# Heads of the blocks in a two-layer f32 kernel: weights split across block ends, the second unit's low part by GpSimd, and the norm's root later

## The reference, cut to what matters

```python
def rms_norm_2(x, g):
    xf = x.astype(jnp.float32)
    y = xf * lax.rsqrt(jnp.mean(xf * xf, axis=-1, keepdims=True) + EPS)
    return (y * g.astype(jnp.float32)).astype(x.dtype)

def swiglu(h, w_gate, w_up, w_down):
    return (jax.nn.silu(h @ w_gate) * (h @ w_up)) @ w_down
```

## Time and profile before

| | us |
|---|---|
| median of three runs | 1918.85 |
| the profiled execution | 1918.93 |
| its span, first to last instruction | 1917.1 |
| PE busy in the span | 1732.8 (90%) |
| DVE busy | 1429.0 (75%) |
| ACT busy | 612.9 (32%) |
| POOL busy | 371.2 (19%) |

### The profile page before, as it was taken

How to read it: one execution, slowest core, us unless ns; L and a number is a source line. 1 busy time by engine, 2 the same in 40 slices (tenths; PEclk the granted TensorE clock), 3 DMA queues, 4 the chain that set the end, 5 groups by cost and what they waited for, 6 DMA issues and landing times.

```text
span 1917.1 us, 25162 instructions
## 1 busy us (share of the span) xinstructions
PE 1732.8 (90%) x9676; PEld 1319.2 (69%) x9676; DVE 1429.0 (75%) x2702; ACT 612.9 (32%) x798; POOL 371.2 (19%) x324
## 2 busy tenths in 40 slices
PE   6999988777787877878999998999999999989999
PEld 4788853333333323336999898899989997779998
DVE  7887789888888888877888778655565656866554
ACT  2135331010100011002643413554454444455452
POOL 0002145444445444451000054000000000000000
PEclk9999999998989898899999999999999999999999
DMA  9856599999999999996545453554545454444543
GB/s 394 317 204 234 196 393 409 422 422 421 422 421 421 422 422 416 421 398 259 190 170 201 162 198 111 186 188 177 194 165 192 176 190 155 153 155 153 186 178 118
DMA packets 68600, 508.57 MB, mean 265 GB/s; under 512 B 7777, under 2 KB 12129, under 8 KB 15969
## 3 DMA queue, kind: packets, MB, share of 16 engines
q0 software_dynamic: 37008, 268.98, 34.0%
q1 hardware_dynamic: 25920, 230.45, 32.6%
q10 hardware_dynamic: 5584, 7.98, 1.3%
HBM read 505.28 MB, written 6.29 MB: 267 GB/s over the span
## 4 chain that ended last, share of the span: by engine, by line
PE 62%; DMA 15%; DVE 15%; ACT 2%; issue 2%; POOL 2%; ACTq 1%; SPq 0%; DVEq 0%; POOLq 0%
PE PB L943 24%; PE PB L954 11%; PE PB L925 11%; DMA arena<-in_uv,eidx 9%; DMA ring<-in_uv,eidx 6%; PE PB L1129 2%; PE PB L666 2%; PE PB L737 2%; DVE arena L1758 1%; PE PB L618 1%; PE PB L723 1%; PE PB L834 1%; DVE gu_lo L1312 1%; PE PB L970 1%; PE PB L856 1%
## 5 line engine op out<-in xcount | busy, mean ns | idle before, releaser
L925 PE MATMUL PB<-arena 128*128 128x512 f32 x604 | 304.9, 663 | 96.5 <-DVE arena L1780 96.5
L943 PE MATMUL PB<-h_hi,gu_hi 128*128 128x256 f32 x1344 | 377.6, 281 | 3.5 <-DVE gu_lo L1846 3.4
L943 PE MATMUL PB<-h_hi,gu_lo 128*128 128x256 f32 x1344 | 376.9, 280 | 0.0
L943 PE MATMUL PB<-h_lo,gu_hi 128*128 128x256 f32 x1344 | 375.8, 280 | 0.0
L925 PEld LDWEIGHTS PB<-arena 128*128 128x128 f32 x604 | 125.2, 212 | 275.0 <-issue 149.6
L2775 POOL DMA_INDIRECT arena<-in_uv,eidx x193 | 225.7, 1170 | 319.5 <-PE PB L925 218.5
L1758 DVE CUSTOM_DVE_ANT_0 arena<-arena,XN 128x1024 f32<-128x1024 f32 x187 | 222.9, 1222 | 60.8 <-DMA arena<-in_uv,eidx 60.7
L943 PEld LDWEIGHTS PB<-h_hi,gu_hi 128*128 128x128 f32 x1344 | 254.1, 189 | 8.0 <-DVE gu_lo L1846 5.1
L943 PEld LDWEIGHTS PB<-h_lo,gu_hi 128*128 128x128 f32 x1344 | 252.0, 188 | 2.8
L943 PEld LDWEIGHTS PB<-h_hi,gu_lo 128*128 128x128 f32 x1344 | 252.7, 188 | 0.0
L1846 DVE TENSOR_TENSOR gu_lo<-ring,gu_hi 128x2048 fp32r<-128x2048 f32 x84 | 192.5, 2292 | 16.4 <-ACT gu_hi L2514 14.4
(11 more groups left out here) (460 smaller groups left out, 2974.1 us busy)
## 6 DMA issues: line engine op xcount, KB each, us to landing
ring<-in_ffn SPq DMA_DIRECT2D x88, 1536.0 KB, 6.7
arena<-in_ada SPq DMA_DIRECT2D x24, 768.0 KB, 8.1
ring<-in_qkv SPq DMA_DIRECT2D x12, 1024.0 KB, 4.7
ring<-in_zg SPq DMA_DIRECT2D x8, 1024.0 KB, 4.9
ring<-in_ada SPq DMA_DIRECT2D x4, 1536.0 KB, 13.8
ring<-in_up SPq DMA_DIRECT2D x4, 1024.0 KB, 4.8
ring<-in_wo SPq DMA_DIRECT2D x4, 1024.0 KB, 6.6
ring<-in_pq SPq DMA_DIRECT2D x4, 1024.0 KB, 4.8
```

Of the source, the lines that this page charges most:

```text
L925: mm = pe.matmul(PB[2 + 2 * t + h][:, :], lhsT=diag(n), rhs=uv[n % UVB][:, 1, h * 512:(h + 1) * 512], start=False, stop=False, skip_group_ ...
L943: mm = pe.matmul(PB[j % 2][:, b * T:(b + 1) * T], lhsT=w[:, j % 2, o:o + P], rhs=h[:, k, :], start=(k == 0 and m == 0), stop=(k == DC - 1 ...
```

## The change

1. **Weights split on across block ends.** ACT casts the next block's units 0 and 1 behind the silus of the last two units (`next_block`, `lead_next_block(f, j)`); behind a mixer it casts unit 1 when the mixer's last output unit is done. DVE makes unit 0's low part ahead of the last unit's `scale_gate`, no longer behind the last `activation`.
2. **The second unit's low part by POOL** (`split_second`, `trail` in the POOL program) in ffn1, ffn2, ffn3, S5 and the attention mixer. In ffn0 DVE still makes it, now ahead of the sum of squares.
3. **Activations first.** ACT writes all of `h_hi`, then squares, then takes the root (ffn0: casts unit 1 between). DVE makes all of `h_lo`, then `norm_sums`, the inverse root and the diagonals.
4. **The root's row inside the second unit.** PE makes it between the gate's half and the up half of gate_up(1) (not for S5, where its place is kept). DVE makes the down weights' low part of unit 0 ahead of keeping the row.
5. The first two and last four units of ffn1 to ffn3 are written out, so the loop holds 16.

```diff
-                root_row(n, 6)
-                rolled = LOOPS if f else 0
+                gate_up(1, between=lambda: root_row(n, 6))
+                down(0)
+                gate_up(2)
+                down(1)
...
             def head(n):
 
+                split_pairs(n, 0, 1, 2, 3)
                 norm_sums(n)
-                split_pairs(n, 0, 1)
                 norm_root(n)
-                split_pairs(n, 2)
-                if n in DG:
-                    diagonals()
-                split_pairs(n, 3)
+                diagonals()
...
                 else:
-                    split_pairs(n, 0, 1)
+                    split_pairs(n, 0, 1, 2, 3)
+                    split_gate_up(1)
                     norm_sums(n)
-                    split_pairs(n, 2, 3)
                     norm_root(n)
                     diagonals()
-                split_gate_up(1)
                 link(v.tensor_scalar(stat[:, 12:14], stat[:, 6:8], 0.5, None, ALU.mult))
+                split_down(0)
                 keep_root_row(n, 6)
...
+                    if j == FU - 2:
+                        if f == 0:
+                            trail("s5in", 0)
+                        elif f == 1:
+                            split_next_block(2)
+                        elif f == 2:
+                            trail("qkv", 0)
                 dve.wait_ge(a_done, a0 + FU + 2)
...
+            def head(n):
+
+                tell(s.activation(stat[:, 14:15], ones[:, 0:1], ACT.Sqrt), act_link)
+                split_h(n)
+                square(n)
+                norm_root(n)
...
                 if f == 0:
                     tell(s.activation(stat[:, 14:15], ones[:, 0:1], ACT.Sqrt), act_link)
-                    split_h(n, 3)
+                    split_h(n)
                     act.wait_ge(uv_used, TT * NSLOT)
+                    lead_gate_up(1)
+                    norm_root(n)
...
                     if j + 2 < FU:
                         lead_gate_up(j + 2)
+                    else:
+                        next_block(j + 2 - FU)
...
-            act.wait_ge(unit_done, UNIT[("s5out", 2)] + 1)
-            lead_next_block(1)
+            for j in range(2):
+                act.wait_ge(unit_done, UNIT[("s5out", 2 + j)] + 1)
+                lead_next_block(1, j)
...
+            def split_second(f):
+
+                pool.wait_ge(gu_hi_done, FU * f + 2)
+                pool.wait_ge(gu_lo_done, FU * f + 1)
+                g.tensor_tensor(gu_lo[:, 1, :], ring[:, (ffn_base[f] + 1) % NS, 0:2 * D], gu_hi[:, 1, :].bitcast(F32),
+                                ALU.subtract).then_inc(gu_lo_done, 1)
+                pool.wait_ge(gu_lo_done, FU * f + 2)
```

More of the change, by code:

```diff
@@ L939, in gate_up @@
                     for b in range(2):
+                        if b:
+                            between()
                         for k in range(DC):
@@ L983, in ffn @@
                 clear(3)
-                root_row(n, 6)
-                rolled = LOOPS if f else 0
-                if rolled:
-                    with pe.Fori(0, rolled) as i:
-                        for j in range(NS):
+                gate_up(1, between=lambda: root_row(n, 6))
+                down(0)
+                gate_up(2)
+                down(1)
+                if f:
+                    with pe.Fori(0, ROUNDS) as i:
+                        for j in range(2, 2 + NS):
                             gate_up(j + 1, i)
                             down(j, i)
-                for j in range(rolled * NS, FU):
+                for j in range(2 + ROUNDS * NS if f else 2, FU):
                     if j + 1 < FU:
@@ L1873, in ffn @@
                 else:
-                    split_pairs(n, 0, 1)
+                    split_pairs(n, 0, 1, 2, 3)
+                    split_gate_up(1)
                     norm_sums(n)
-                    split_pairs(n, 2, 3)
                     norm_root(n)
                     diagonals()
-                split_gate_up(1)
                 link(v.tensor_scalar(stat[:, 12:14], stat[:, 6:8], 0.5, None, ALU.mult))
+                split_down(0)
                 keep_root_row(n, 6)
[L1882 to L1885, removed]
+                scale_gate(0)
+                activation(0)
+                dve.wait_ge(gu_lo_done, a0 + 2)
+                split_gate_up(2)
+                scale_gate(1)
+                split_down(1)
+                activation(1)
+                if f == 0:
+                    s5_tables(1)
+                split_gate_up(3)
+                if f:
+                    with dve.Fori(0, ROUNDS) as i:
+                        for j in range(2, 2 + NS):
                             scale_gate(j, i)
@@ L2522, in silu, with next_block @@
                     s.activation(act_gs[:, j % 2, :], act_gs[:, j % 2, :], ACT.Silu).then_inc(silu_done, 1)
+                def next_block(j):
+                    if f == 1:
+                        lead_next_block(2, j)
+                    elif f < 3:
+                        lead(("s5in", None, "qkv")[f], j, a_done, FU * (f + 1) + 1 + j)
                 if f == 0:
                     tell(s.activation(stat[:, 14:15], ones[:, 0:1], ACT.Sqrt), act_link)
[L2527 removed]
+                    split_h(n)
                     act.wait_ge(uv_used, TT * NSLOT)
[L2529 to L2536 removed]
+                    lead_gate_up(1)
+                    norm_root(n)
+                else:
+                    head(n)
+                if f:
+                    for j in range(2):
+                        lead_down(j)
+                        silu(j)
+                        lead_gate_up(j + 2)
+                    with act.Fori(0, ROUNDS) as i:
+                        for j in range(2, 2 + NS):
                             lead_down(j, i)
@@ L2539, in ffn @@
                             lead_gate_up(j + 2, i)
-                for j in range(rolled * NS, FU):
+                for j in range(2 + ROUNDS * NS if f else 0, FU):
                     lead_down(j)
@@ L2718, in _ @@
             lead("mo", 3, unit_done, UNIT[("mo", 1)] + 1)
-            act.wait_ge(unit_done, UNIT[("mo", 2)] + 1)
-            lead_next_block(3)
+            for j in range(2):
+                act.wait_ge(unit_done, UNIT[("mo", 2 + j)] + 1)
+                lead_next_block(3, j)
             ffn(3)
```

89 lines of the change are left out of this document (32 added, 57 removed).

## The result

The changed kernel takes 1925.8 us (median of 6 executions) against 1918.9 for the kernel before; the ratio is 1.0042, with an interval of 1.0031 to 1.0054. It is slower, as forecast (1924.8, range 1920.0 to 1928.3). The profiled execution took 1925.62 us with a span of 1923.8; before it was 1918.93 and 1917.1.

What follows compares the result with a forecast made beforehand. PE carries 62% of the chain; only its waits in the heads were taken to matter. Terms 4.36 + 1.75 + 1.75 - 0.7 - 0.7 - 0.6 = +5.86 on 1918.93 give 1924.8 us, range 1920.0 to 1928.3.

Steps and rivals of the forecast that it cites:

- ffn0's scaled gate: ffn0's head: DVE's new order moves the scaled gate from 898.10 to 902.46, +4.36 us, and gate_up(3) with it.
- Either way this costs nothing more: ffn0: whether or not POOL's zeroing holds the a_hi cast, PE's chain ends inside gate_up(3)'s start at 922.2; 0 extra.
- The rival on the clock: PE idling ahead of ffn0's down(0) and ffn1's and ffn3's first matmuls lowers its clock: +3.3 us, 1928.1; chance 0.10.
- PE's row is ready by then: ffn0: PE's root row inside gate_up(1) is ready when DVE's down weights' subtraction ends at 902.00, adding no delay.
- ffn1 and ffn3, +1.75 each: Heads of ffn1 and ffn3: ACT's unit 1 cast, table load and small root go ahead of h_hi; +1.75 us each.
- S5, ffn2, attention: -0.7, -0.7, -0.6: Heads of S5, ffn2 and attention: PE's next work starts earlier by 0.7, 0.7 and 0.6 us.
- POOL's low part: 0: Second unit's low part on POOL, taken as 5.1 us, ends before gate_up(1) needs it in ffn1; worth 0.
- the shared-port rival: POOL's new subtraction meeting DVE's sum of squares would cost up to 1.2 us a head; within the range, no chance given.
- The thin covers: Around the row in gate_up(1) and unit 2's low part, work stays hidden by 0.2 and 0.15 us; otherwise some tenths per head.

Runs made afterwards that it cites:

- ffn0_row_ahead: Changed kernel with ffn0's new order kept on DVE and ACT, but PE's root row ahead of gate_up(1): 1923.2 us, ratio 1.0029.
- ffn0_row_inside: Changed kernel with ffn0's old order on DVE and ACT only, PE's root row staying inside gate_up(1): 1924.7 us, ratio 1.0028.
- memset_later: Changed kernel with POOL's zeroing in ffn0 waiting for a_done 1, a count already met, so the zeroing did not move: 1925.1 us, ratio 1.0035.
- zeroing_behind_a: Changed kernel with POOL's zeroing in ffn0 behind a_lo of unit 0, by the right count (a_done 3): 1927.4 us, ratio 1.0033.
- gains_alone: Changed kernel with the heads of ffn0, ffn1 and ffn3 put back to the old order; S5, ffn2 and attention heads stay changed: 1916.4 us, ratio 0.9982.
- gains_split: gains_alone with only ACT's 16 transfers in ffn0 parted in eight and eight: 1914.8 us, ratio 0.9981.
- gains_zero_split: gains_alone with two edits in ffn0, the zeroing behind a_lo of unit 0 and ACT's 16 transfers parted in eight and eight: 1912.7 us, ratio 0.9963.

## Why the prediction was right, step by step

- **ffn0's scaled gate**, +4.36: measured +4.26. The subtraction began at 893.70 + 1.46 = 895.16 (895.18 forecast), the squares at 897.36 (897.4), the inverse root 1.77 behind them (1.83).
- **"Either way this costs nothing more"** was wrong. The cast was held as forecast and down(0) started where it was put (909.4 for 909.5), but the forecast gave down(0) 2.9 us behind 5 us of idle time. At 1.2 GHz it took 5.1, and PE became later than the transfers by about 1.4 us. The transfers in their turn took 0.7 us less, and by them alone the delay of gate_up(3) would have been about 3.6 us, not 4.4; with the clock it was 4.9. The two errors go against each other, and that 4.4 came so near is luck. ffn0_row_ahead, with down(0) at full clock, gives 1.05 us of it back. The rival on the clock had this place and called it covered but for a little.
- **"PE's row is ready by then"** is true and hid a second cause. In the sum all 4.36 us are DVE's order. ffn0_row_inside shows that the row's place alone makes the same delay at gate_up(3); the sum was right because the two run side by side and don't add up.
- **ffn1 and ffn3, +1.75 each**: it was +1.76 and +1.75 in the heads, with `h_hi` 3.45 us behind the last unit (3.42) and PE's wait at 2.38 (2.4). The clock rival came true in ffn3, +1.46, and not in ffn1.
- **S5, ffn2, attention: -0.7, -0.7, -0.6.** In the heads -0.60 to -0.67, -0.59 and -0.31. Attention is mis-sized by half: the forecast took the shorter chain off PE's wait, but the wait only went from 1.26 to 1.23 us, and the gain is no more than what the transposes now end earlier. The diagonals of S5 do come last (0.19 us of waiting), and the path over them, which the forecast worked out as 0.57 us before it took 0.7, was the one to go by: the unit behind the row starts 0.60 us earlier.
- **POOL's low part: 0.** It took 4.55 us where 5.1 was taken from the row of 512 columns, ended at 1228.77 and was wanted at 1233.66. The sum of squares began at 1230.49, so the two didn't meet, and no run tests what the shared-port rival says of that pair. The Trainium skill's GPSIMD Engine Reference (3.1, elementwise) has 4.5 us for an elementwise operation of this shape, and the trace agrees.
- **The thin covers** held: in ffn1's and ffn3's heads of the changed kernel gate_up(2) starts about 0.1 us later than it would unhindered, and nothing waits behind it.

The terms give +5.86; by the stages the change cost 8.2 us in this execution (6.7, and 1.47 given back ahead of ffn0), of which 1.46 are ffn3's clock and 1.0 the end. What is left is 5.7. So the terms were right but for what follows ffn0's scaled gate, and what the sum lacks is mostly the clock, which the forecast had as a rival of 0.10 and not as a term. That the time lies only 1 us from the forecast owes something to luck as well: in the profiled execution the store's 1.0 us and the 1.47 ahead of ffn0, neither of them shown to be the change's doing, nearly cancel. The Trainium skill (TensorE: Matmul & The Clock Gate, Part 1) says that an idle engine falls to half rate. The runs bear that out behind every wait of 4.1 us and more in ffn0, and behind waits of 2.4 us only in 3 of 14 cases.

## What to carry over

Read a wait on PE together with what is late behind it: in ffn0 three things (a held cast, ACT's transfers, the clock) stood one behind the other, taking the first away moved the idle time to the next, and only two edits at once paid in full. When an operation that waits is put ahead of others in an engine's program order, everything behind it is released by that wait too: the early cast in ffn1 and ffn3 drew the table load and the small root behind the wait, and issuing these two ahead of it gave back 1.6 of the 1.75 us although the cast stayed. And where three heads gain and three lose, take the change apart by head: half of it was worth keeping. A median that comes out as forecast doesn't show that each stage did; here stages that an edit leaves alone moved by up to 3.0 us from one profile to the next.

## What the runs showed of the hardware

The clock of PE falls behind some waits and not behind others of the same length. Seven kernels have a wait of 2.36 to 2.39 us ahead of the first matmuls of ffn1 and of ffn3, 14 in all. At three of them the granted clock fell and 48 matmuls took about 7.4 us for 5.9: ffn3 in the changed kernel and in memset_later, ffn1 in zeroing_behind_a. None of twelve such places with a wait of 0.61 to 0.77 us showed it. With the waits of 4.1 to 5.3 us in ffn0 it fell every time (seven of seven). Why it falls behind one wait of 2.37 us and not behind another stays open.

A fall costs PE from 1.0 us (gate_up(1) in ffn0_row_ahead) to 3.0 (ffn0_row_inside: down(0) took 5.5 us for 2.9 and gate_up(2) 6.1 for 5.65), one or two heads' worth. What the kernel pays hangs on where it comes: ahead of a wait for another engine it is covered. The S5 mixer has such a fall in all thirteen profiles. In four of them (ffn0_row_ahead, gains_alone, gains_split, gains_zero_split) it comes ahead of PE's last wait for POOL, which is then 1.55 to 1.81 us, and the mixer takes 130.2 us; in the nine others it comes within that wait, then of 3.2 us, or at its end, and the mixer takes 131.5 to 132.5.

Falls also come and go in stages whose code is the same. The attention mixer took 120.2 to 120.6 us in seven of the thirteen profiles, with no fall, and 121.9 to 122.65 in the six others, whose edits lie elsewhere. In all six the granted clock fell behind a wait of 1.9 us for DVE, and in four of them again behind the next long one, of 2.3 us (122.6 us for 121.9).

The zeroing on POOL held the cast to `a_hi` on DVE in each kernel in which they met, from 4.6 to 5.2 us for 0.29, to its end. The big subtraction that met the zeroing in zeroing_behind_a was not held (2.29 us there too). POOL's subtraction of two inputs beside DVE's `h_lo` cost DVE nothing (3.84 us for 3.85). Whether it cost POOL anything no run shows: the subtraction took 4.5 to 4.6 us beside `h_lo` in every head, and none has it alone.
